# Row-maximum products one step earlier in two softmax attentions, and the first row transposition moved into the last gate block

## The reference, cut to what matters

```python
proj = h @ w_in
cq, ckv, k_rope, fq, fk, fv, f_logit, g_mla, g_fox = split(proj)
# mla: queries and keys of 64 + 32 (rope) channels, from latents
# fox: queries and keys of 64 channels, logit + F[t] - F[s]
for each block of 128 queries:
    logits = q @ k.T * scale (+ F[t] - F[s] for fox)
    p = softmax(where(key <= query, logits, -inf))
    out = p @ v
y = sigmoid(g_mla) * (o_mla @ w_o_mla) + sigmoid(g_fox) * (o_fox @ w_o_fox)
```

## Time and profile before

| what | us |
|---|---|
| median of 3 runs (lowest, highest) | 3079.42 (3075.91, 3080.59) |
| the profiled execution's own time | 3078.65 |
| its span, first to last instruction | 3076.9 |
| PE busy in the span | 2952.5 (96%) |
| DVE, ACT, POOL busy | 1580.1, 795.4, 1042.4 |
| fox attention in the span | about 1756 to 1910 |
| mla attention in the span | about 1969 to 2149 |

### The profile page before, as it was taken

The page is one execution under the profiler, slowest core; times in us unless marked ns, Lnnn a source line. Parts: engine busy times, 40 slices in busy tenths (PEclk is TensorE's granted clock), DMA queues, the critical chain, the costliest instruction groups (busy, mean ns, idle before and its releaser), DMA issues.

```text
span 3076.9 us, 34139 instructions
## 1 busy us (share of the span) xinstructions
PE 2952.5 (96%) x13230; PEld 2345.1 (76%) x13230; DVE 1580.1 (51%) x1566; ACT 795.4 (26%) x1062; POOL 1042.4 (34%) x466
## 2 busy tenths in 40 slices
PE   6999998899999999899999999999998999999998
PEld 5876676688888888677888866766886888888886
DVE  3629954734555555873332165555545333343356
ACT  2128953311212221331002133234013111111112
POOL 2330023344444444234444430410442344444342
PEclk9999999999999999899999989999999999999999
DMA  2121032112222222221313343421321111111112
GB/s 109 48 76 24 5 123 76 42 69 96 95 95 95 95 97 73 90 97 49 116 69 123 111 95 124 107 49 45 148 88 41 48 48 48 48 48 48 48 48 75
DMA packets 84976, 232.99 MB, mean 76 GB/s; under 512 B 19280, under 2 KB 27728, under 8 KB 84112
## 3 DMA queue, kind: packets, MB, share of 16 engines
q1 hardware_dynamic: 79584, 211.49, 20.9%
q10 hardware_dynamic: 5296, 20.19, 1.6%
HBM read 176.26 MB, written 28.05 MB: 66 GB/s over the span
## 4 chain that ended last, share of the span: by engine, by line
PE 72%; issue 12%; DVE 5%; POOL 2%; ACT 1%; DMA 0%; SPq 0%; POOLq 0%; DVEq 0%; ACTq 0%
PE ps L350 57%; PE ps L1219 3%; PE ps L2319 2%; PE ps L2292 2%; PE ps L1996 1%; PE ps L2333 1%; DVE stick_sp L971 1%; PE ps L2709 1%; POOL w_lo L318 1%; PE ps L403 1%; POOL w_hi L315 1%; DVE stick_sp_hi L982 1%; DVE stick_a L995 1%; PE ps L3197 1%; PE ps L1551 0%
## 5 line engine op out<-in xcount | busy, mean ns | idle before, releaser
L315 POOL TENSOR_TENSOR w_hi<-w_raw,inv_count 128x1024 fp32r<-128x1024 f32 x194 | 372.1, 1918 | 1653.5 <-PE ps L350 1011.7
L318 POOL TENSOR_TENSOR w_lo<-w_raw,w_hi 128x1024 fp32r<-128x1024 f32 x194 | 517.4, 2667 | 15.2
L350 PE MATMUL ps<-x_hi,w_hi 128*128 128x512 f32 x1152 | 359.4, 393 | 16.0 <-POOL w_lo L318 9.9
L350 PE MATMUL ps<-x_hi,w_lo 128*128 128x512 f32 x1152 | 356.9, 391 | 0.0
L350 PE MATMUL ps<-x_lo,w_hi 128*128 128x512 f32 x1152 | 356.8, 391 | 0.0
L350 PEld LDWEIGHTS ps<-x_hi,w_hi 128*128 128x128 f32 x1152 | 218.1, 190 | 64.1 <-issue 12.8
L350 PEld LDWEIGHTS ps<-x_lo,w_hi 128*128 128x128 f32 x1152 | 217.7, 189 | 45.7
L350 PEld LDWEIGHTS ps<-x_hi,w_lo 128*128 128x128 f32 x1152 | 217.7, 189 | 45.5
L350 PE MATMUL ps<-hidden_hi,w_lo 128*128 128x512 f32 x800 | 246.3, 389 | 0.0
L350 PE MATMUL ps<-hidden_hi,w_hi 128*128 128x512 f32 x800 | 246.3, 389 | 0.0
L350 PE MATMUL ps<-hidden_lo,w_hi 128*128 128x512 f32 x800 | 246.3, 389 | 0.0
(11 more groups left out here) (420 smaller groups left out, 5098.9 us busy)
## 6 DMA issues: line engine op xcount, KB each, us to landing
w_raw<-wall SPq DMA_DIRECT2D x217, 512.0 KB, 3.2
ada_raw<-wada SPq DMA_DIRECT2D x48, 512.0 KB, 4.2
gates_scratch<-gate_out ACTq DMA_DIRECT2D x16, 512.0 KB, 2.6
gate_in<-gates_scratch SPq DMA_DIRECT2D x8, 1024.0 KB, 7.4
residual<-x_t SPq DMA_DIRECT2D x8, 512.0 KB, 9.2
residual<-x_t SPq DMA_DIRECT2D x2, 2048.0 KB, 9.4
emb_scratch<-emb_out ACTq DMA_DIRECT2D x8, 512.0 KB, 2.6
embedding<-emb_scratch SPq DMA_DIRECT2D x2, 2048.0 KB, 12.5
```

The source lines that it names most:

```text
L315: nc.gpsimd.tensor_tensor(w_hi[:, slot, :], w_raw[:, slot, :], one.to_broadcast([P, S]), ALU.mult).then_inc(w_split, 1)
L318: nc.gpsimd.tensor_tensor(w_lo[:, slot, :], w_raw[:, slot, :], w_hi[:, slot, :].bitcast(F32), ALU.subtract).then_inc(w_split, 1)
L350: last = nc.tensor.matmul(ps[:, banks + c, :], lhs, x[:, k0 + k, c * HALF:(c + 1) * HALF], start=k == 0 and n == 0, stop=k == nk - 1 and n ...
```

## The change

1. `maxes_to`: steps 0 and 1 of a pair bring the pair's total to 10 and 12 (before: 8, 10 and 12 in steps 0, 1 and 2), and the products of the next pair begin in step 4 (before: 5). It is used by fox and by mla.
2. The last gate block is cut after 2, and again after 6, of its 8 parts (before: after 4). Products 2 and 3 stand in the first cut, `rows(0)` of fox in the second.
3. ACT makes fox's first `row_copy` ahead of the last gate's sigmoid, its store and the table load. mla keeps its first rows where they were.

```diff
-        for g in range(8, N_GATES):
+        for g in range(8, N_GATES - 1):
             gate(g)
+        with after(IN2):
+            fox.row_copy(act, 0)
+        gate(N_GATES - 1)
         load_exp_ln()
...
-        product(pe, b % 2, 0, 8, x_hi, x_lo, 0, 6, range(4))
+        product(pe, b % 2, 0, 8, x_hi, x_lo, 0, 6, range(2))
         with after(IN2):
             fox.largest(pe, 2)
             fox.largest(pe, 3)
-        product(pe, b % 2, 0, 8, x_hi, x_lo, 0, 6, range(4, 8)).then_inc(w_used, 1)
+        product(pe, b % 2, 0, 8, x_hi, x_lo, 0, 6, range(2, 6))
+        with after(IN2):
+            fox.rows(pe, 0)
+        product(pe, b % 2, 0, 8, x_hi, x_lo, 0, 6, range(6, 8)).then_inc(w_used, 1)
...
-        own = 8 + 2 * min(r, 2)
-        return min(12 * p + own + max(0, r - 4), len(MAXES))
+        own = 10 + 2 * min(r, 1)
+        return min(12 * p + own + max(0, r - 3), len(MAXES))
...
-            for m in range(done, 4):
-                self.largest(pe, m)
-            self.rows(pe, 0)
+            if done < 5:
+                self.rows(pe, 0)
...
-            row_copy(0)
+            if not done:
+                self.row_copy(act, 0)
...
-        fox.scalar(act, also)
+        fox.scalar(act, also, 1)
...
-        fox.tensor(pe, 4)
+        fox.tensor(pe, 5)
...
-        mla.scalar(act, also)
+        mla.scalar(act, also, 0)
```

More of the change, by code:

```diff
@@ L2363, in tensor, with row_copy, scalar @@
                     sums(u)
[L2365 to L2371, removed]
+        def row_copy(self, act, u):
+            act.wait_ge(*row_full.at(u + 1))
+            for h in range(2):
+                r = 32 + 64 * h
+                nc.scalar.activation(self.row_out(u // 2, h)[:, (u % 2) * HALF:(u % 2 + 1) * HALF],
+                                     ps[r:r + 4, self.bank("row", u), :], ACT.Copy).then_inc(row_done.sem, 1)
+        def scalar(self, act, also, done):
             def exp(k):
@@ L2388, in inverse @@
                 nc.scalar.activation(self.inv[:, :], self.inv[:, :], ACT.Exp, scale=-1.0).then_inc(inv_done.sem, 1)
-            row_copy(0)
+            if not done:
+                self.row_copy(act, 0)
             for s in range(NA + 3):
                 for u in rows_due(s):
-                    row_copy(u)
+                    self.row_copy(act, u)
                 if s < NA:
```

## The result

| what | before | after |
|---|---|---|
| median of 4 runs (lowest, highest), us | 3079.36 (3075.91, 3080.59) | 3107.78 (3105.57, 3110.16) |
| profiled execution, own time and span | 3078.65, 3076.9 | 3106.54, 3104.8 |
| PE busy | 2952.5 | 2969.1 |
| last gate block, fox and the latents | 230.2 | 228.7 |
| mla, first scores to last values | 173.7 | 202.3 |

The change makes the kernel slower: 28.4 us, ratio 1.0095 (95% interval 1.0081 to 1.0108). The forecast was 3085.8 with a range from 3077 to 3092; it was wrong. The three stages come from the timeline of PE: from fox's first row-maximum product to mla's first scores, and from there to the start of mla's last value products. Fox gave 1.5 us, mla took 28.6, the rest 0.8.

A forecast was written before the change was run, and what follows sets the result against it. PE was taken as busy almost throughout, with about 14 us of idle time and some low clock within reach. The terms summed to +7.1 us on the profiled 3078.65, giving 3085.8 us, range 3077 to 3092.

The forecast's parts named there:

- Fox, start: Start of fox: the 2.08 us wait for ACT's row copy becomes a wait for product 12's copies; -0.5 us.
- its other units: Fox's later units: three 0.8 us waits on the negated maxima go; -2.4 us.
- Mla, pair 1: Mla, pair 1: rows start 2.3 us earlier, but PE waits 4.7 us for the query copies; -0.2 us.
- that rule: DVE and POOL block each other by issue order; in mla's pair 1, copies 1.9 us later, total +9; not taken.
- Mla, pair 2: Mla, pair 2: rows gain nothing, copies land later and PE waits 3.1 us; +3.95 us, between +1 and +5.
- pair 3: Mla, pair 3: rows come 0.73 us earlier, but PE waits 3.7 us for copies; +2.95 us, 0 to +4.
- the last unit's -0.7: Mla's last unit: no pair follows, so its wait on the negated maxima goes; -0.7 us.
- The clock: Low PE clock after mla's three new waits: three times 0 to 2.9 us, 1.3 taken each; +4 us.
- rival C: Clearly slower: low clock after new waits lasts as in fox's 24 us, one or two places; +5 to +8, 3092; chance 0.13.
- Rival A: Faster: the copies do not bind in mla and waits on the maxima shrink; -9.5, 3069 us; chance 0.12.
- Rival B: Same: waits trade places at no new clock cost, or copies land 2 us sooner; +3, 3081.7 us; chance 0.20.
- Rival D: The gate block's part cannot be seen, its 2 us being behind the copies anyway; moves nothing; no chance given.

The follow-up runs named there:

- e9: The changed kernel with 31, 18 and 20 extra matrix products in mla's three new waits for copies; 3086.03 us, ratio 1.0035.
- e12: The changed kernel with mla's query splits sooner: pair 1 both in step 0, pairs 2 and 3 in steps 8, 9 and 20, 21; 3068.47 us.
- e2: The changed kernel with the old table in fox and mla, keeping only the gate block's part; 3076.90 us, ratio 0.9998.
- e15: e10 without the gate block's part of the change; 3068.67 us, ratio 0.9964.
- e10: e12 with the next pair's products from step 5 instead of 4 in both attentions; 3065.51 us, ratio 0.9964.
- e14: The changed kernel with 10 extra 512-column products directly behind each of mla's three waits for copies; 3112.84 us, ratio 1.0101.
- e1: The changed kernel with the old table in mla only; fox and gate block stay changed; 3076.87 us, ratio 0.9997.
- e4: The changed kernel with 24, 14 and 14 extra matrix products in mla's three new waits for copies; 3098.72 us, ratio 1.0067.
- e5: The changed kernel with mla's query splits for pairs 2 and 3 in steps 8, 9 and 20, 21, pair 1 left; 3078.75 us, ratio 1.0002.
- e3: The changed kernel with the next pair's products from step 5 instead of 4 in both attentions; 3086.90 us, ratio 1.0030.
- e11: e1 with fox's next-pair products from step 5 instead of 4; 3073.03 us, ratio 0.9986.

## Why the prediction was wrong, point by point

- **Fox, start: -0.5, and its other units: -2.4.** PE idled 8.0 us as forecast, but in two pieces: 2.8 at the rows of unit 1, 5.2 for the copies of `forget_rows`. The forecast lacked the first: PE came to the rows of unit 1 at full clock and ahead of DVE. The three 0.8 us waits went. The stage became 1.5 us shorter, not 2.9; it stayed within its bounds.
- **Mla, pair 1: -0.2.** The mechanism was right, the wait mis-sized: 6.7 us for 4.7. Mla started 0.8 us sooner than in the rows I worked from, so DVE was at `q_rope_low` at 1983.56 and not at 1984.5, about on time when counted from mla's first scores. POOL's split came 1.3 us sooner than in the earlier trace rows, at 1983.40, and so 0.16 us ahead of it. This is the case that I weighed and did not take: by the Trainium skill (SBUF, State Buffer, "Who interferes with whom") the later one waits for the shared ports, and `q_rope_low` took 2.82 us. Counted from mla's first scores product 12 started 1.9 us later than forecast, 1.5 us by `q_rope_low`'s later end and 0.4 by slower copies; I had 1.9 us for that rule. This is all of the missing 2 us of wait. By that rule I had +9 for the sum, still far from +28.
- **Mla, pair 2: +3.95, pair 3: +2.95.** Waits of 3.9 and 3.8 us where I had 3.1 and 3.7. Before pair 2 the rows did wait for the end of POOL's splits, as I had it: 2.1 us, where my times hold 2.6 without naming them as a wait. The 0.7 us at the sums I did not have. With the last unit's -0.7, mla was to lose 6.0 us without the clock; by e9 it lost 9.5.
- **The clock: +4. This is the step that failed.** "Three times 0 to 2.9; I take 1.3 each" took its size from one short stretch after a 3.22 us wait, and called 2.9 the bound. It was 19.1 us, some 6 each: the clock stayed low for 13.7 to 15.7 us with PE at work, not for 6. The reason given for taking less than half of the bound, "the work there is partly bound by ACT", fails as well: from 2055 to 2068 PE was busy 13.00 of 13.00 us. The stretch of 24 us in the earlier trace rows, behind a wait of 2.08 us, stood in the same rows; I gave it to rival C, in "one or two places" and with 0.13. It came in all three, so even C's 3092 was too low. The range had no reason to end there: by the same arithmetic three stretches as long as fox's would cost up to 12 us each. Of the 21 us between forecast and result the clock is 15, the waits of mla 3.5, fox 1.4.
- **Rival A** fell as expected: the copies bind. Yet its size was about right for what the copies held back: with them in time the kernel gains 9 us by the ratio, 10 by the medians (e12), though e12 has moved the splits as well.
- **Rival B** (no cost of the clock) has its answer in e9: even with the clock kept full, it is slower than before, by 0.35%.
- **Rival D**: the traces of e2 and e15 show that the gate block's part acts on the waits and on the clock; on the time of e2 it didn't show.
- Of what would show it wrong, "low clock of more than 10 us in one piece" came true, three times in mla and once in fox (17.1 us).

## What to carry to other kernels

When work on the critical engine is taken forward, list what stands behind it on the helper engines' queues: here one small split, `q_rope_low`, fell behind two more reductions and into POOL's split. With all of the splits moved ahead, +0.95% became -0.30% (e12: 3068.5 us, nothing else changed), and -0.36% with the later start step as well (e10: 3065.5 us, some 1.3% below the change). Bound the price of a new idle time on PE by the longest low stretch in the trace and not by a short one: here the three waits of 4 to 7 us and what came with them cost 9.5 us themselves and 19.1 us by the clock; the stretch of 6 us gave a bound of 8.7 us, fox's stretch of 24 us gives 36. And where two stages share a table, test it in each: (10, 1, 4) was better than (10, 1, 3) by 3 to 4 us in fox; in mla it was 15 us better with the late splits and the same with the early ones.

## What was not expected of the hardware

- In the changed kernel PE stayed at 1.2 GHz for 14 to 16 us while it was busy without a gap (1995 to 2010, 2055 to 2068, 2107 to 2122), after idle times of 3.8 to 6.7 us; in e14 it was 20.4 us (2055 to 2075). The Trainium skill (TensorE: Matmul & The Clock Gate, "What's actually happening") has it that "activity releases the throttle". The trace agrees in that the full clock came back in every stretch, in some after 3.4 to 7 us; but it shows 14 us and more of work without a gap at the lower level first.
- The length repeats with the order of the work: fox with the start in step 4 had a stretch of 17.1 us in each of seven profiles (the changed kernel, e1, e4, e5, e9, e12, e14), with the start in step 5 one of 10.2 us in each of three (e3, e10, e11). Mla with the table of before varied more: 6.8 and 3.4 us in the kernel before, 6.8 and 6.8 in e1, 3.4 and 3.4 in e2 and e11.
- An idle time of 1.3 us was followed by 13.6 us of low clock in e4, one of 2.8 us in e10 by 3.4.
- Ten products of 512 columns right behind the idle time (e14) did not bring the clock back sooner; the same kind of product in the idle time (e9) kept it up.
- A DVE operation of 8 elements a row (L2428 in e10; 0.17 us at the same place in the changed kernel) took 1.66 us when it began 0.27 us after a POOL operation on SBUF, and ended with it, at 1980.6.
